# Preparing RWKV pairs 2 to 4 of a hybrid decoder step on GpSimd instead of VectorE

## The reference

```python
xs = cols + (prev - cols) * mu                 # token shift
r, k, v = xs[..., :W], xs[..., W:2 * W], xs[..., 2 * W:3 * W]
w_log = -jax.nn.softplus(-(w0 + jnp.tanh(wd) @ w2)) - 0.5
decay = jnp.exp(-jnp.exp(w_log))
a = jax.nn.sigmoid(a0 + ad @ a2)
kk = k * k_k
k = k * (1.0 + (a - 1.0) * k_a)
kk = kk / jnp.maximum(jnp.linalg.norm(kk, axis=-1, keepdims=True), 1e-12)
...                                            # per step t:
    sa = jnp.einsum('bhvk,bhk->bhv', S, -kkt)
    S = S * wt[:, :, None, :] + sa[..., None] * (kkt * at)[:, :, None, :] + vt[..., None] * kt[:, :, None, :]
y = head_norm(ys, gn_g, GN_EPS) + gn_b
y = y + (jnp.sum(r * k * r_k, axis=-1, keepdims=True) * v).reshape(B, T, W)
```

## Time and profile before

| what | value |
|---|---|
| median of three runs | 2252.91 us (2242.82 to 2256.2) |
| profiled execution, its own time | 2249.52 us |
| its span | 2247.8 us |
| its mean granted TensorE clock | 0.946 |
| four RWKV pairs in it | 342 to 616 us |

### The profile page before, as it was taken

How to read it: one execution, slowest core, us unless ns; L and a number is a source line. 1 busy time by engine, 2 the same in 40 slices (tenths; PEclk the granted TensorE clock), 3 DMA queues, 4 the chain that set the end, 5 groups by cost and what they waited for, 6 DMA issues and landing times.

```text
span 2247.8 us, 35701 instructions
## 1 busy us (share of the span) xinstructions
PE 2085.7 (93%) x14513; PEld 1829.3 (81%) x14513; DVE 1578.2 (70%) x2758; ACT 752.2 (33%) x921; POOL 452.7 (20%) x395
## 2 busy tenths in 40 slices
PE   7998877777899998999999999999999999999995
PEld 7987656666745777888888889989899999999995
DVE  6435656666522888978888898887776667776664
ACT  5234334333202002334444544455322222222221
POOL 8111100000000000022242232213333333322220
PEclk9998867777899999999999999999999999999998
DMA  5122110002022212467798788778988888888872
GB/s 183 57 60 56 50 36 2 7 2 82 14 95 92 68 45 100 172 233 264 262 337 306 265 308 311 257 265 331 369 333 322 315 303 305 309 306 309 309 254 91
DMA packets 175771, 437.45 MB, mean 195 GB/s; under 512 B 12192, under 2 KB 92832, under 8 KB 165280
## 3 DMA queue, kind: packets, MB, share of 16 engines
q1 hardware_dynamic: 127552, 242.81, 31.2%
q0 software_dynamic: 36864, 134.23, 16.1%
q10 hardware_dynamic: 11232, 58.73, 6.4%
HBM read 368.57 MB, written 67.17 MB: 194 GB/s over the span
## 4 chain that ended last, share of the span: by engine, by line
PE 58%; DVE 11%; issue 1%; ACT 1%; DMA 0%; POOL 0%; ACTq 0%; DVEq 0%
PE bank L1728 28%; PE bank L1666 22%; PE bank L1675 3%; PE bank L1593 3%; DVE sc L2269 1%; DVE si L2268 1%; DVE si L2271 1%; DVE isel L2411 1%; DVE sv L2267 1%; DVE sv L2270 1%; DVE u_lo L2276 1%; DVE sca L2282 1%; DMA sca<-in_pu_rows,pick 0%; ACT u_hi L1026 0%; PE bank L1647 0%
## 5 line engine op out<-in xcount | busy, mean ns | idle before, releaser
L1666 PE MATMUL bank<-xhi,u_hi 128*128 128x448 f32 x1024 | 386.3, 377 | 9.6 <-DVE u_lo L2276 9.0
L1728 PE MATMUL bank<-w_hi,v_hi 128*128 128x448 f32 x1024 | 375.0, 366 | 5.5 <-DVE w_lo L2514 5.5
L1666 PE MATMUL bank<-xhi,u_lo 128*128 128x448 f32 x1024 | 376.0, 367 | 0.0
L1666 PE MATMUL bank<-xlo,u_hi 128*128 128x448 f32 x1024 | 375.1, 366 | 0.0
L1728 PE MATMUL bank<-w_lo,v_hi 128*128 128x448 f32 x1024 | 374.9, 366 | 0.0
L1728 PE MATMUL bank<-w_hi,v_lo 128*128 128x448 f32 x1024 | 374.8, 366 | 0.0
L688 POOL DMA_INDIRECT sca<-in_pu_rows,pick x128 | 171.7, 1341 | 731.8 <-DVE sdot L2282 445.6
L688 POOL DMA_INDIRECT rows_v<-in_pv,pick x128 | 197.4, 1542 | 429.4 <-DVE xs L2496 379.4
L2520 DVE TENSOR_TENSOR v_lo<-v_raw,v_hi 128x4096 fp32r<-128x4096 f32 x32 | 141.6, 4425 | 170.9 <-ACT v_hi L1087 170.9
L1087 ACT ACTIVATE v_hi<-v_raw 128x4096 fp32r<-128x4096 f32 x32 | 116.1, 3627 | 428.7 <-PE bank L1728 411.7
L1666 PEld LDWEIGHTS bank<-xhi,u_hi 128*128 128x128 f32 x1024 | 193.1, 189 | 24.8 <-issue 8.5
(11 more groups left out here) (577 smaller groups left out, 3446.1 us busy)
## 6 DMA issues: line engine op xcount, KB each, us to landing
u_raw<-in_pu SPq DMA_DIRECT2D x64, 1024.0 KB, 5.1
v_raw<-in_pv SPq DMA_DIRECT2D x32, 2048.0 KB, 16.9
act_scratch<-actb ACTq DMA_DIRECT2D x64, 448.0 KB, 5.9
gate_scratch<-gst ACTq DMA_DIRECT2D x14, 2048.0 KB, 9.2
wts<-act_scratch SPq DMA_DIRECT2D x32, 896.0 KB, 4.8
gring<-gate_scratch SPq DMA_DIRECT2D x32, 896.0 KB, 8.7
wring<-in_w_q SPq DMA_DIRECT2D x4, 2048.0 KB, 9.1
wp_raw<-in_w_in SPq DMA_DIRECT2D x7, 1024.0 KB, 5.5
```

What stands on the lines that cost most here:

```text
L1666: ins = mm(bank[b][:, 0:DS], lhsT, rhs[:, 0:DS], **on)
L1728: ins = mm(bank[c][:, 0:DS], lhsT, rhs[q][:, e, :], **on)
```

## The change

For pairs p = 1 to 3 the preparation becomes a program of GpSimd, in a row and without steps. It starts when the pair before has its bonus (and, where the buffers were used by pair p - 2, when that one's results are copied) and otherwise waits for its data alone. [...] VectorE keeps the running sum and difference, the reciprocal, the kk product (now with a minimum of 1e12 in place of the clamp), AR's first half and the EpE copies; they stand earlier in the steps than they did. ScalarE takes the root straight from PSUM, in two instructions. TensorE waits for `kk_norm` where it waited for `kk_clamped`. The first pair keeps its way as `prep_first`; `kk_clamped` is renamed `kk_stage`.

```diff
 @@ GpSimd, behind the scaling @@
+            def prep(p):
+                P, AR = XP[p % 2], ARP[p % 2]
+                TT, TSC = pool.tensor_tensor, pool.tensor_scalar
+                def shifted(dst, tmp, ct):
+                    seq = [a.rearrange("p (b s) -> p b s", b=NB) for a in (ext_r[:, ct, 1 + SEQ:], tmp[:, SEQ:NT], dst[:, SEQ:NT])]
+                    cur, prev = ext_r[:, ct, 1:1 + SEQ], ext_r[:, ct, 0:SEQ]
+                    TT(tmp[:, 0:SEQ], prev, cur, ALU.subtract)
+                    link(TT(seq[1], seq[0][:, :, 0:NS], seq[0][:, :, 1:], ALU.subtract))
+                    link(TSC(tmp[:, :], tmp[:, :], pcol("mu", ct), None, ALU.mult))
+                    TT(dst[:, 0:SEQ], tmp[:, 0:SEQ], cur, ALU.add)
+                    link(TT(seq[2], seq[1], seq[0][:, :, 1:], ALU.add))
+                pool.wait_ge(S("bonus_ready"), p)
+                if p >= 2:
+                    pool.wait_ge(S("gh_copied"), 2 * p - 2)
+                    pool.wait_ge(S("sample_copied"), 3 * p - 3)
+                be, ka, t = P["be"], P["ka"], X["t"]
+                shifted(X["k"], be, 4 + p)
+                link(TSC(X["kk"][:, :], X["k"][:, :], pcol("k_k", p), None, ALU.mult))
+                TT(t[:, :], X["kk"][:, :], X["kk"][:, :], ALU.mult).then_inc(S("kk_squares"), 1)
+                shifted(X["r"], ka, p)
+                shifted(P["v"], be, 8 + p)
+                pool.wait_ge(S("lora_out"), 2 * p + 2)
+                link(TSC(ka[:, :], X["av"][:, :], 1.0, pcol("k_a", p), ALU.subtract, ALU.mult))
+                link(TSC(ka[:, :], ka[:, :], 1.0, None, ALU.add))
+                link(TT(X["k"][:, :], ka[:, :], X["k"][:, :], ALU.mult))
+                pool.wait_ge(S("kk_stage"), p + 1)
+                link(TT(be[:, :], X["kk"][:, :], X["av"][:, :], ALU.mult))
+                pool.wait_ge(S("decay_ready"), p + 1)
+                TT(be[:, :], be[:, :], X["En"][:, :], ALU.mult)
+                TT(ka[:, :], X["k"][:, :], X["En"][:, :], ALU.mult)
+                TT(AR[:, 1, :], X["r"][:, :], X["cum"][:, :], ALU.mult)
+                link(TSC(t[:, :], X["r"][:, :], pcol("r_k", p), None, ALU.mult))
+                pool.wait_ge(S("ar_ready"), p)
+                TT(t[:, :], t[:, :], X["k"][:, :], ALU.mult).then_inc(S("chan_ready"), 1)
+            for p in range(1, 4):
+                prep(p)
 @@ ScalarE, kk_root @@
-                act.wait_ge(S("kk_clamped"), p + 1)
-                act.activation(X["t"][:, :], X["t"][:, :], ACT.Sqrt).then_inc(S("kk_norm"), 1)
+                if p:
+                    act.wait_ge(S("kk_summed"), p + 1)
+                    act.activation(X["t"][:, 0:SEQ], bank[4][:, :], ACT.Sqrt)
+                    act.activation(X["t"][:, SEQ:NT], rest_of(4), ACT.Sqrt).then_inc(S("kk_norm"), 1)
 @@ TensorE, post @@
                     if p < 2 and c == 4:
-                        pe.wait_ge(S("kk_clamped"), p + 3)
+                        pe.wait_ge(S("kk_norm"), p + 3)
 @@ VectorE, the whole of the new prep; what it replaces stands above @@
+            def prep(p):
+                AR = ARP[p % 2]
+                yield
+                yield
+                decay_sums(p)
+                yield
+                decay_diff(p)
+                yield
+                yield
+                dve.wait_ge(S("kk_norm"), p + 1)
+                link(dve.reciprocal(X["t"][:, :], X["t"][:, :]))
+                yield
+                STT(out=X["kk"][:, :], in0=X["t"][:, :], scalar=1e12, in1=X["kk"][:, :], op0=ALU.min, op1=ALU.mult
+                    ).then_inc(S("kk_stage"), 1)
+                own(S("kk_stage"))
+                yield
+                dve.wait_ge(S("decay_ready"), p + 1)
+                STT(out=AR[:, 0, :], in0=X["kk"][:, :], scalar=-1.0, in1=X["sw"][:, :], op0=ALU.mult, op1=ALU.mult)
+                dve.tensor_copy(EpE[:, p, 0:8], X["cum"][:, RCH - 1:SEQ:RCH])
+                dve.tensor_copy(EpE[:, p, 8:16], X["cum"][:, SEQ + NS - 1:NT:NS]).then_inc(S("ar_ready"), 1)
+                own(S("ar_ready"))
+                for _ in range(11):
+                    yield
+                bonus(p)
+                yield
```

More of the change, by code:

```diff
@@ L788, in kk_root @@
             def kk_root(p):
-                act.wait_ge(S("kk_clamped"), p + 1)
-                act.activation(X["t"][:, :], X["t"][:, :], ACT.Sqrt).then_inc(S("kk_norm"), 1)
+                if p:
+                    act.wait_ge(S("kk_summed"), p + 1)
+                    act.activation(X["t"][:, 0:SEQ], bank[4][:, :], ACT.Sqrt)
+                    act.activation(X["t"][:, SEQ:NT], rest_of(4), ACT.Sqrt).then_inc(S("kk_norm"), 1)
+                else:
+                    act.wait_ge(S("kk_stage"), 1)
+                    act.activation(X["t"][:, :], X["t"][:, :], ACT.Sqrt).then_inc(S("kk_norm"), 1)
                 own(S("kk_norm"))
@@ L1312, in _ @@
             numerators(3)
-            pe.wait_ge(S("kk_clamped"), 1)
+            pe.wait_ge(S("kk_stage"), 1)
             job(next(jobs))
@@ L1884, in kk_clamp @@
                     last = TS_(dst, src, 1e-24, None, ALU.max)
-                last.then_inc(S("kk_clamped"), 1)
-                own(S("kk_clamped"))
+                last.then_inc(S("kk_stage"), 1)
+                own(S("kk_stage"))
             def decay_sums(p):
@@ L1895, in decay_diff, with bonus, prep_first @@
                 own(S("cum_ready"))
-            def prep(p):
-                P, AR = XP[p % 2], ARP[p % 2]
+            def bonus(p):
+                dve.wait_ge(S("bonus_done"), p + 1)
+                for dst, src, v in zip(main_samp(mixT[:, 4 + p, :]), (bank[4][:, :], rest_of(4)), main_samp(XP[p % 2]["v"])):
+                    last = TT(dst, src, v, ALU.mult)
+                last.then_inc(S("bonus_ready"), 1)
+                own(S("bonus_ready"))
+            def prep(p):
+                AR = ARP[p % 2]
[11 more added lines that the diff above has]
+                    ).then_inc(S("kk_stage"), 1)
+                own(S("kk_stage"))
+                yield
[8 more added lines that the diff above has]
+                yield
+            def prep_first():
+                p, P, AR = 0, XP[0], ARP[0]
                 link(shifted(X["r"], p))
@@ L1907, in prep @@
                 yield
[L1908 to L1920, removed]
+                decay_sums(0)
+                decay_diff(0)
+                yield
+                kk_clamp(0, 0)
+                yield
                 dve.wait_ge(S("kk_norm"), p + 1)
@@ L1925, in prep @@
                 dve.wait_ge(S("lora_out"), 2 * p + 2)
-                if p == 0:
-                    dve.wait_ge(s_pj, NJ)
+                dve.wait_ge(s_pj, NJ)
                 link(shifted(P["v"], 8 + p))
@@ L1947, in prep @@
                 own(S("chan_ready"))
[L1948 to L1954, removed]
+                yield
+                bonus(0)
                 yield
@@ L1981, in _ @@
             own(S("tails_ready"))
-            early = prep(0)
+            early = prep_first()
             dve.wait_ge(s_pe, NF)
```

3 lines of the change are left out of this document (1 added, 2 removed).

## The result

| what | before | after |
|---|---|---|
| median (range), 17 runs each | 2252.91 us (2242.82 to 2261.71) | 2228.78 us (2220.07 to 2246.24) |
| ratio of the two, 95% interval | | 0.9908 (0.9889 to 0.9927) |
| profiled execution, its own time | 2249.52 us | 2228.57 us |
| its span, mean granted clock | 2247.8 us, 0.946 | 2226.7 us, 0.956 |

What follows compares the result with a forecast made beforehand. No engine was full: VectorE, TensorE and ScalarE hand a chain to and fro. Minus 8.3 plus 2.0 in pair 0, and twice minus 3.8 plus 3.8, gave minus 6.3 from 2249.52: 2243 us, range 2228 to 2264.

Steps and rivals of the forecast that it cites:

- Pair 0, minus 8.3 free of contention: Pair 0: shifts and key work leaving VectorE shorten it by 8.3 us, before any charge for GpSimd contention.
- Up to the s=1 additions: Pair 0: M 4.1 us earlier, but the reciprocal now ahead; additions start at 364.0 instead of 364.62.
- I give 0.5: Pair 0, first merge: some 4 us of VectorE work go, but TensorE and ScalarE need nearly as long; 0.5 us gained.
- Contention in pair 0, plus 2.0: Pair 0: only AR0 and the EpE copies pay for GpSimd's work beside VectorE, 2.0 us.
- Pairs 1 and 2, order: Pairs 1 and 2: waiting for the root and reciprocal starts the s=1 additions 3.6 us later; net still minus 3.8 each.
- Pairs 1 and 2, plus 3.8 of contention each: Pairs 1 and 2: decay_sums 1.2, AR0 and EpE copies 2.0, second SsS 0.6 us lost beside GpSimd.
- Pair 2, zero: Pair 2: a gain of 3.8 us and contention of 3.8 us cancel, so no change.
- Pair 3, zero: Pair 3: it prepares no successor, so its length does not change.
- the price of tensor_scalar: GpSimd's program: a 128x576 tensor_scalar takes 1.0 us, bounded by 0.58 and 1.40.
- the cover of 5.5 us: Pair 0: GpSimd's second part ends at 374.0, 5.5 us before TensorE needs it at 379.5.
- Rival 3: All pairs: GpSimd needs twice the assumed prices beside VectorE, TensorE waits in pair 0; plus 14, 2264 us, chance 0.13.
- Rival 1: Pairs 0 to 2: VectorE's load bounds, order and contention cost nothing; 2223 to 2225, with order 2234; chance 0.17.

Runs made afterwards that it cites:

- e8: Kernel before, with five idle TensorE products (results unread) in pair 0's wait for the M masks; four pairs sum to 268.0 us against 273.7.
- e4: Changed kernel with GpSimd's preparation of pairs 1 to 3 left out, six memsets a pair in its place, output not the reference's; 2240.14 us.
- e7: Kernel before, everything still on VectorE, with the preparation of pairs 1 to 3 put in the change's order; 2250.38 us.
- e1: Changed kernel with the clamp back on VectorE for pairs 1 to 3, ScalarE's root again one instruction from SBUF; 2230.25 us, ratio to before 0.9918.
- e2: Changed kernel with reciprocal and kk product two calls later, behind the s=1 additions, in pairs 1 and 2; 2245.31 us, ratio to before 0.9975.
- e3: Changed kernel with both the clamp back on VectorE and the reciprocal two calls later in pairs 1 and 2; 2231.23 us, ratio to before 0.9925.
- e6: Changed kernel with the two EpE copies of pairs 1 to 3 moved from VectorE to ScalarE; 2241.07 us, ratio to before 0.9958.
- e9: Changed kernel with three idle TensorE products (results unused) at the end of each of pairs 0 to 2; 2244.59 us.
- e10: Changed kernel with the clamp back on VectorE only for the preparation that runs in pair 1; 2232.19 us, ratio to before 0.9919.
- e12: Changed kernel with idle 256-column TensorE products at two places inside pairs 1 and 2; 2233.05 us, ratio to before 0.9927.
- e5: Changed kernel with four more 128x576 GpSimd products ahead of the second part of its program; 2238.25 us.
- e15: Kernel before, with idle TensorE products at three places in pair 0: wait for M, ahead of s=3, ahead of first merge; pair 0 60.2 us.

## Why the prediction was wrong

The forecast was 6.3 us, in the pairs 20.5 were measured. The step that failed is one that the sum never took. It read a granted clock of 0.78 and then kept TensorE's durations as the trace had them, which puts the clock's share at nothing without a reason. The runs showed 3.0 us of clock behind M in pair 0 (e8), some part of 2.6 more at the first merge, and 6.8 in pair 2. Term by term:

- **Pair 0, minus 8.3 free of contention:** three of its terms were off. Up to the s=1 additions I had 0.6 and it was 3.8. This is where the step fails first: I took the a product and the sum's product at 2.1 us each, and with the shorter wait for M they are 1.1. e8 gives 3.0 for it with VectorE's load unchanged. From there to TensorE's start on the merges I had 7.2 and it was 6.3. Here the clock took something back: behind its new wait of 4.01 us for the s=1 additions TensorE ran the s=2 products at the lower level (0.45 and 0.66 us, 0.31 and 0.42 before), and the last s=2 addition waited 0.76 for them. From there to the second merge I had "I give 0.5" and it was 3.1. That TensorE needs nearly as long as VectorE there was true at the clock of 0.55 (5.97 of 6.45 us busy) and false at 1.00 (2.76).
- **Contention in pair 0, plus 2.0:** zero by e4. The collisions are there (EpE 1.37), but in front of s=2 additions the last of which waits for TensorE anyway.
- **Pairs 1 and 2, order:** right. s=1 additions later by 4.0 for 3.6, link c=4 held by the root for 2.95, e7's 3.7 and 3.6 for the order. The s=2 additions were not: I had them 0.8 later and they came 3.9 later, because AR0 waits for ScalarE's exponentials until 426.69 (34.8 into the pair, where I had 32.7) and EpE pays 1.2 behind it.
- **Pairs 1 and 2, plus 3.8 of contention each:** 2.3 in pair 1 by e4; in pair 2 the clock covers it, and the sum is as before. That pair 1 came out at minus 0.7 for a forecast of 0 is two errors against each other: minus 3.0 without GpSimd where I had minus 3.8, plus 2.3 where I had 3.8.
- **Pair 2, zero:** minus 6.8. It is TensorE's clock, 0.86 for 0.74; at 0.78 the code of before and the changed code take 78.1 and 78.0. That the change hit on the higher clock there is luck as far as the forecast goes. Which instruction of pair 1 sets it up isn't settled: e1, e2, e3, e6, e9 and e10 each lost it, e12 kept it.
- **Pair 3, zero:** right, 0.2.
- **GpSimd:** the price of tensor_scalar was beyond my upper bound. It cost nothing, but the cover of 5.5 us was 1.3. Both parts were nearly a third longer than I had, yet `chan_ready` came 1.0 earlier; the cover went because TensorE came to the bonus product at 374.3 and not at 379.5. Rival 3's mechanism was 1.3 us away in pair 0, and e5 sets it off.
- **Rival 1** (VectorE's load is the bound, 2223 to 2234) is the nearest in time. Its 10.6 at most for pair 0 are near the 10.2 that needed the load off, though these had the clock's help; but the 8 us that it counted in each of pairs 1 and 2 did not come: the order and the root's wait kept them, and the clock gave 6.8 in one of the two.

The ledger: 8.3 forecast in pair 0, plus 3.2 up to s=1, minus 0.9 up to the merges, plus 2.6 there, is 13.2; plus 0.7 in pair 1, plus 6.8 in pair 2, minus 0.2 in pair 3: 20.5.

## What to carry to other kernels

Where the granted clock is well below 1 in a stage, read the durations of TensorE there at both levels: a shortened wait of TensorE may also halve the products behind it, and two stages with the same code can differ by 6 us on that alone. A higher clock is worth something only where TensorE is on the path (e8 yes, e15 no), and where TensorE and VectorE are both nearly full, as in the first merge, load off one and clock on the other pay only together. Judge a removed instruction by whether the engine that carries it has a gap ahead of the next shared step, and an added engine by its cover in the first stage that needs it.

## What the runs showed of the hardware

- GpSimd's tensor_scalar of 128x576 fp32 took 1.66 to 1.74 us with one operation (up to 2.67 where VectorE's work fell beside it) and 2.2 with two, a tensor_tensor of the same size mostly 1.15 to 1.46: the form with one tensor is the slower one.
- An 8-column copy on VectorE took 1.37 us beside a GpSimd product (0.17 in the kernel before), once in each pair: a short instruction can pay a whole long one.
- Less work for VectorE made pairs longer (e6, e4's pair 2). With equal code the length followed the granted clock from 73.1 at 0.86 to 79.3 at 0.76 (pair 2, the changed kernel and e10).
- Behind one and the same wait of 2.06 us, sixteen 128x128 transposes took 1.94 us in one kernel and 3.54 in another with the same code there: the wait just ahead does not tell the level; what came earlier counts too.
